# A mixer whose attention rows of two chunks are turned in slot 11, with the output products begun beside the first scores

## What is computed

```python
def parallel_mixer(x, pos, w_in, gate_bias, conv_w, conv_b, sink, att_g, mlstm_g, w_out):
    u = x @ w_in
    aq, ak, av = ...          # 8 query heads, 2 key/value heads of 64, rotated in part
    y_att = rms_norm(windowed_gqa(aq, ak, av, sink), att_g)
    y_ml = mlstm_group(u_qk, u_v, u_o, u_gates, ...)   # 4 heads of 128, both directions
    return concatenate([y_att, y_ml], axis=-1) @ w_out
```

## Time and profile before

| what | value |
|---|---|
| time, median of 3 runs | 2205.72 us (2204.82 to 2207.74) |
| time of the profiled execution | 2197.67 us |
| its span | 2196.1 us |
| mean granted clock of TensorE | 0.984 |
| PE busy | 2095.0 us, 10880 matmuls |
| DVE busy | 1318.4 us (60%) |
| ACT busy | 979.1 us (45%) |
| POOL busy | 226.7 us (10%) |

### The profile page before, as it was taken

One profiled execution on the slowest core, in us unless ns is written; L12 is line 12 of the kernel. 1 busy time (PEld: TensorE's weight loads), 2 busy tenths in 40 slices (PEclk: granted clock), 3 DMA queues, 4 the chain that ended last, 5 costly groups with the idle time before them and its releaser, 6 DMA issues.

```text
span 2196.1 us, 30246 instructions
## 1 busy us (share of the span) xinstructions
PE 2095.0 (95%) x10880; PEld 1671.8 (76%) x10880; DVE 1318.4 (60%) x2005; ACT 979.1 (45%) x1570; POOL 226.7 (10%) x268
## 2 busy tenths in 40 slices
PE   7999999999999899999799998999999989999998
PEld 6888767878877677777588886788888767777774
DVE  3785577721455765556868647782335476665567
ACT  3554565232422355455246547523333134555553
POOL 0000032000001321000100002300000042100004
PEclk9999999999999999999899999999999999999999
DMA  4163202321103699999511112123210169999996
GB/s 156 58 226 128 103 30 79 114 86 49 58 29 125 247 367 373 387 383 346 198 59 39 39 39 96 44 112 115 77 58 20 41 228 384 373 375 373 380 382 230
DMA packets 78526, 384.78 MB, mean 175 GB/s; under 512 B 10472, under 2 KB 11864, under 8 KB 43608
## 3 DMA queue, kind: packets, MB, share of 16 engines
q1 hardware_dynamic: 55264, 327.31, 39.5%
q0 software_dynamic: 10096, 30.38, 3.8%
q10 hardware_dynamic: 13064, 25.75, 3.2%
HBM read 352.27 MB, written 46.07 MB: 181 GB/s over the span
## 4 chain that ended last, share of the span: by engine, by line
PE 79%; DVE 12%; ACT 6%; issue 2%; DMA 1%; DVEq 0%; ACTq 0%; POOL 0%; SPq 0%; POOLq 0%
PE bank L2247 32%; PE bank L2781 10%; PE bank L2755 9%; PE bank L2745 7%; PE bank L2482 5%; PE bank L2454 2%; PE bank L2592 2%; PE bank L2513 2%; PE bank L2268 2%; DVE weight_slots_parts L1472 1%; PE bank L2721 1%; PE bank L2636 1%; DVE weight_slots_parts L1953 1%; PE bank L2652 1%; PE bank L2422 1%
## 5 line engine op out<-in xcount | busy, mean ns | idle before, releaser
L1953 DVE TENSOR_TENSOR weight_slots_parts<-weight_slots,mixer_region_parts 128x2048 fp32r<-128x2048 f32 x140 | 323.4, 2330 | 85.1 <-ACT mixer_region_parts L1296 85.0
L2247 PE MATMUL bank<-weight_slots_parts,x_transposed_parts 128*128 128x512 f32 x864 | 278.6, 404 | 1.4 <-DVE weight_slots_parts L1472 1.4
L1296 ACT ACTIVATE mixer_region_parts<-weight_slots 128x2048 fp32r<-128x2048 f32 x140 | 260.9, 1908 | 23.4 <-ACT x_transposed L1371 18.1
L2247 PE MATMUL bank<-x_transposed_parts,weight_slots_parts 128*128 128x512 f32 (+1 forms) x1024 | 260.7, 341 | 3.8 <-DVE mixer_region_parts L1441 2.7
L1472 DVE TENSOR_TENSOR weight_slots_parts<-weight_slots,weight_slots_parts 128x2048 fp32r<-128x2048 f32 x58 | 132.9, 2292 | 197.5 <-ACT weight_slots_parts L981 196.6
L2781 PE MATMUL bank<-weight_slots,x_transposed 128*128 128x512 f32 x560 | 247.6, 595 | 0.0
L2755 PE MATMUL bank<-mixer_region_parts,x_transposed_parts 128*128 128x256 f32 x1120 | 207.5, 284 | 1.1 <-DVE weight_slots_parts L1953 1.1
L2247 PEld LDWEIGHTS bank<-x_transposed_parts,weight_slots_parts 128*128 128x128 f32 x1024 | 178.5, 191 | 25.9 <-issue 3.6
L2745 PE MATMUL bank<-mixer_region_parts,x_transposed_parts 128*128 128x512 f32 x560 | 192.2, 414 | 5.4 <-ACTq L1336 2.4
L2781 PEld LDWEIGHTS bank<-weight_slots,x_transposed 128*128 128x128 f32 x560 | 104.1, 191 | 118.5 <-issue 102.9
L2247 PEld LDWEIGHTS bank<-weight_slots_parts,x_transposed_parts 128*128 128x128 f32 x864 | 162.3, 194 | 33.8 <-DVE weight_slots_parts L1472 2.3
(11 more groups left out here) (322 smaller groups left out, 3525.4 us busy)
## 6 DMA issues: line engine op xcount, KB each, us to landing
weight_slots<-in_w_gate SPq DMA_DIRECT2D x70, 1024.0 KB, 7.4
weight_slots<-in_w_up SPq DMA_DIRECT2D x70, 1024.0 KB, 7.2
weight_slots<-in_w_down SPq DMA_DIRECT2D x70, 1024.0 KB, 8.0
weight_slots<-in_w_in SPq DMA_DIRECT2D x20, 1024.0 KB, 5.2
slots_y<-x_transposed ACTq DMA_DIRECT2D x66, 256.0 KB, 7.2
weight_slots<-in_wkv_mem SPq DMA_DIRECT2D x16, 1024.0 KB, 4.8
slots_y<-in_consts SPq DMA_DIRECT2D x6, 2304.0 KB, 16.9
weight_slots<-in_w_out SPq DMA_DIRECT2D x8, 1024.0 KB, 4.9
```

What stands on the lines that cost most here:

```text
L1296: nc.scalar.activation(hi, raw, ACT.Copy).then_inc(moe.high_ready, 1)
L1953: v.tensor_tensor(lo, raw, hi.bitcast(F32), ALU.subtract).then_inc(moe.low_ready, 1)
L2247: ins = pe.matmul(ps, lhs[i](k), rhs[j](k), start=k == 0 and a == 0, stop=k == KD - 1 and a == 2)
```

## The change

- The scores of three key blocks take four banks, one head of 384 columns in each; there is no second group behind the turned probabilities. The stream tiles have banks 6 and 7 while such slots are ahead.
- Slot 11 has three stream tiles and slot 12 one, ("o", 5, 1), between the spread maxima and the weighing. ScalarE's sigmoid of ("o", 4, 1) moves behind group 0, beside that of ("o", 5, 1).
- The roots are taken in slot 9 for chunks 0 to 2, whose rows are scaled at the end of VectorE's slot 9, and in slot 11 for chunks 3 and 4.
- wo0 is split one tile earlier. Attention rows of chunks 0 and 1 are turned in slot 11 into banks 0 and 1, behind the weighing, and split there.
- Group 0 does two steps of the early sums behind each of its four scores, none behind the first score of group 1, and one at each point from then on. Rows of chunks 2 to 5 are turned in group 0 into banks 5 and 6. VectorE adds nothing to the residual in group 0.

```diff
-PER_SLOT = [3, 3, 2, 3, 3, 2, 4, 4, 4, 4, 4, 4]
+PER_SLOT = [3, 3, 2, 3, 3, 2, 4, 4, 4, 4, 4, 3, 1]
-YT_BEHIND = ((), (0, 1, 2, 3), (4,), (5,))
+YT_AHEAD = (0, 1)
+YT_BEHIND = ((), (2, 3), (4,), (5,))
...
 def score_tiles(i):
-    pairs = ((0, 2), (0, 1)), ((1, 3), (0, 1))
-    return pairs if keys_of(GROUP_ORDER[i][0])[1] == 2 else pairs + (((0, 1, 2, 3), (2,)),)
+    return ((0, 2), (1, 3)) if keys_of(GROUP_ORDER[i][0])[1] == 2 else ((0,), (1,), (2,), (3,))
 def stream_banks(i):
-    return (3, 6, 7) if any(len(score_tiles(n)) == 3 for n in range(i, 12)) else (2, 3, 6, 7)
+    return (6, 7) if any(len(score_tiles(n)) == 4 for n in range(i, 12)) else (2, 3, 6, 7)
...
 def early_steps(point):
-    return max(0, ML_POINTS.index(point) + 1 - CHUNKS[0])
+    at = ML_POINTS.index(point)
+    ahead = 4 * len(YT_AHEAD)
+    return min(2 * at + 2, ahead) if at <= CHUNKS[0] else min(ahead + at - CHUNKS[0], EARLY_STEPS)
...
-                add(("sc", i, b), (b,))
+                add(("sc", i, b), (0, 1, 2, 3) if len(score_tiles(i)) == 4 else ((0, 1)[b],))
...
+        for c in YT_AHEAD if i == 11 else ():
+            add(("yt", c, 0), (0, 1))
...
-                    add(("yt", c, 0), (4, 5, 6, 7))
+                    add(("yt", c, 0), (5, 6))
...
+SPLIT_BEHIND[("o", 5, 0)] = SPLIT_BEHIND.pop(("o", 3, 1))
...
# ScalarE
-                        if i == 11:
-                            rstd(st[:, 20:25], st[:, 20:25], 5, 1.0 / ATT, eps_rms).then_inc(att_rs, 1)
+                        if i in (9, 11):
+                            lo, hi = (20, 23) if i == 9 else (23, 25)
+                            rstd(st[:, lo:hi], st[:, lo:hi], hi - lo, 1.0 / ATT, eps_rms).then_inc(att_rs, 1)
...
                             stream_tile(t)
+                            if t == STREAM[STARTS[11]]:
+                                for c in YT_AHEAD:
+                                    high_x(("yt", c, 0), c, 0)
...
-                                    for c in ((), (0, 1), (2, 3, 4), (5,))[sc]:
+                                    for c in ((), (2,), (3, 4), (5,))[sc]:
                                         high_x(("yt", c, 0), c, 0)
                         if g == 0:
+                            stream_tile(STREAM[-2])
                             stream_tile(STREAM[-1])
...
# VectorE
                         if i == 12:
-                            dve.wait_ge(att_rs, 2 * l + 1)
-                            for c in range(NC - 1):
+                            dve.wait_ge(att_rs, 3 * l + 2)
+                            for c in (3, 4):
                                 attention_scaled(c)
...
                         for t in w[1:]:
                             stream_tile(t)
+                            if t == STREAM[STARTS[11] + 1]:
+                                for c in YT_AHEAD:
+                                    low_y(c, 0)
+                        if i == 9:
+                            dve.wait_ge(att_rs, 3 * l + 1)
+                            for c in range(3):
+                                attention_scaled(c)
...
-                        done_ = early_steps(ML_POINTS[at - 1]) // 4 if at else 0
+                        done_ = early_steps(ML_POINTS[at - 1]) // 4 if point[0] else 0
...
                         if g == 0:
+                            tile_finish(len(STREAM) - 2)
                             tile_finish(len(STREAM) - 1)
...
# TensorE
-                        if i < 12 and nb == 3:
-                            tile_filled(pe, ("pt", i - 1, 0))
-                            scores(2, 1)
-                            scores(2, 3)
+                        if i == 12:
+                            unit_ready("running_max")
+                            spread_maxima(0)
                         if w and i:
                             stream_tile(w[0])
...
+                        for c in YT_AHEAD if i == 11 else ():
+                            pe.wait_ge(y_att, 6 * l + c + 1)
+                            turn4(("yt", c, 0), lambda k: y[:, c, k * P:(k + 1) * P])
                         for t in w[1 if i else 2:]:
                             stream_tile(t)
```

More of the change, by code:

```diff
@@ L135 @@
           + [(name, c, h) for name in ("v", "o") for c0 in (0, 3) for h in range(2) for c in range(c0, c0 + 3)])
-PER_SLOT = [3, 3, 2, 3, 3, 2, 4, 4, 4, 4, 4, 4]
-STARTS = [sum(PER_SLOT[:i]) for i in range(13)]
+PER_SLOT = [3, 3, 2, 3, 3, 2, 4, 4, 4, 4, 4, 3, 1]
+STARTS = [sum(PER_SLOT[:i]) for i in range(14)]
 GATES_TURNED = 8
@@ L1600, in stream_tile @@
                             dve.sem_inc(o_ready, 1)
-                        if i:
+                        if i and key != STREAM[-1]:
                             tile_finish(i - 1)
@@ L1721, in _ @@
                                 if g == 0 and sc == 1:
-                                    dve.wait_ge(att_rs, 2 * l + 2)
+                                    dve.wait_ge(att_rs, 3 * l + 3)
                                     attention_scaled(NC - 1)
                                 if g == 0:
-                                    for c in ((), (0, 1), (2, 3), (4, 5))[sc]:
+                                    for c in ((), (2,), (3, 4), (5,))[sc]:
                                         low_y(c, 0)
@@ L2413, in _ @@
                             tiles = score_tiles(i)
-                            def scores(b, t):
+                            for t in range(GRP):
                                 n, j = head_at(jp, t)
                                 hp = slice(n * HD, (n + 1) * HD)
-                                heads, blocks = tiles[b]
-                                key, at, m = ("sc", i, b), heads.index(t), len(blocks) * P
-                                lo = (k0 + blocks[0]) * P
+                                b = t % len(tiles)
+                                key, at = ("sc", i, b), tiles[b].index(t)
                                 ps = bank_of(key) if at else take(key)
-                                ins = pe.matmul(ps[:, at * m:(at + 1) * m], qT[hp, j, c * P:(c + 1) * P],
-                                                kT[hp, lo:lo + m], start=True, stop=True)
-                                if t == heads[-1]:
+                                ins = pe.matmul(ps[:, at * nb * P:(at + 1) * nb * P], qT[hp, j, c * P:(c + 1) * P],
+                                                kT[hp, k0 * P:(k0 + nb) * P], start=True, stop=True)
+                                if t == tiles[b][-1]:
                                     done(ins, key)
-                            for t in range(GRP):
-                                scores(t % 2, t)
-                            if nb == 3:
-                                scores(2, 0)
-                                scores(2, 2)
                         if i:
```

16 lines of the change are left out of this document (6 added, 10 removed).

## The result

The changed kernel takes 2217.30 us (median, 2212.61 to 2218.35) against 2203.06 of the kernel before: ratio 1.006, 95% interval 1.0044 to 1.0076, or +9.7 to +16.7 us. It is slower, as forecast, but by some 13 us where the prediction had 6.6: twice as much. The forecast of 2212.3 looks nearer than that because it was added to 2205.72, a median of three runs, and the kernel before takes 2203.06 over six. The profiled execution took 2218.35 us.

The account below looks back on a forecast made before the run. TensorE, busy 95%, was taken as the bound, with ScalarE and VectorE setting the pace behind slot 11. -4.8 + 5.35 + 3.65 - 2.8 + 3.4 + 1.8 = +6.6 us, added to 2205.72: 2212.3; range 2204 to 2219.

Parts of the forecast that it names:

- The new wait: Ninth early-sum step, group 0: TensorE stands 6.9 us for VectorE's residual of tile (0, 0), behind decays and two sigmoids.
- The clock behind it: After the idle time at the ninth step the granted clock falls: 1.7 us a layer, +3.4; ends 0 and double.
- Third numerator: Group 0's third numerator tile comes later through TensorE's idle time: +5.35 us in layer 1, +3.65 in layer 0.
- Scores: Slots 2 to 5: four products of 384 columns save 0.6 us a slot, -4.8 over both layers.
- one more pair: Slots 9 to 11: extra tiny ScalarE operations, with three VectorE scalings, are hidden in busy stretches; without that cover 2.3 us.
- Row maxima: Slots 11 and 12: maxima wait about 0.9 us for VectorE's split turned rows, where a wait of 1.4 was.
- the later loads of x: SP's loads of x, wo2 and wo3 start 3 us later, at about 1330: costs nothing, without margin up to 3.
- The tail: Behind group 6's last numerators: TensorE idles about 5 us; -1.4 a layer for earlier output, +0.9 a layer for the clock.
- VectorE starts 1.4 earlier, and so does the first output product: After the last numerators, VectorE's half of wo2 and the first output product come earlier: -1.4 us a layer, -2.8.
- The wait decides, the clock does not: Rival, 25%: everything as forecast but granted clock at 1.00: +1.4 us, 2207.1, within 0.2%.
- The steps fill the gap: Rival, 10%: short wait at the ninth step, -10.6 us or 2195.1; decides once ScalarE's chain is 7 us shorter.
- Low clock for longer: Rival, 10%: twice the forecast's clock terms, 2217.5 us.

Follow-up runs that it names:

- The late sigmoids: Changed kernel with ScalarE's sigmoids of the last two o tiles, and VectorE's products using them, put behind the decays of group 1: ratio 1.0005.
- the filled wait: Changed kernel with 28 needless products of 512 columns ahead of the ninth step, keeping TensorE busy while it would wait: ratio 1.0019.
- the scores alone: Kernel before with only the scores changed (four products of three key blocks, a bank each, stream on two banks): ratio 0.9976, again 0.9974.

## Why the prediction was right, and where its sizes were off

Forecast 2212.3, slower; measured 2217.3, slower, inside the range. The mechanism was the forecast's, the new wait and the low clock behind it; the sum was half of what came. That the time lies within the range is luck in part: the base to which the +6.6 was added was 2.7 us too high, and on a base of 2203.06 the same range would have ended at 2216.3.

| part, both layers | forecast, us | measured, us |
|---|---|---|
| up to slot 11 (scores, slot 9) | -4.8 | -3.3 |
| slot 11 to third numerator (wait, clock) | +12.4 | +16.2 |
| behind it (tail, clock) | -1.0 | +0.3 |
| sum | +6.6 | +13.25 |


- **The new wait.** Forecast 6.9 us, at the ninth step, for the residual of tile (0, 0), in both layers: measured 6.98 and 6.98. Each link of the chain was there in the forecast's order. From slot 11's start TensorE reached the step 0.8 later than forecast (32.84 against 32.01 in layer 1) and ScalarE ended its last high part 0.7 later (32.05 against 31.31), so both ends moved together and the wait kept its size: that it was right to 0.1 is luck, that it was near 7 is not. Of TensorE's 0.8 the prediction's own addition explains 0.3 (1327.5 + 0.7 + 2.8 + 1.7 is 1332.7, not 1332.4). The late sigmoids show the link that matters.
- **The clock behind it** was the term most undersized: 1.7 forecast, from the 2.72 us wait of the earlier trace rows, and 2.9 and 2.6 measured by filling the wait. The idle time here is two and a half times as long, and I took the price of the shorter one. The term lay within its stated ends (0 to double).
- **Third numerator.** With both, +7.05 in layer 1 and +5.35 in layer 0 were forecast from slot 11's start, and +9.14 and +7.06 came: 1.2 and 0.9 of the difference from the clock, 0.9 and 0.8 from the chain being later.
- **Scores.** Forecast -2.4 a layer, measured -2.2 by the end of slot 5: slots 2, 4 and 5 give 0.8 each, and slot 3 gives 0.25 back. There the third turned tile waits for ScalarE's copy of the first, 1.05 us longer than before: TensorE's part of slot 2 has become 0.8 shorter, the chain of VectorE and ScalarE through it has not, and ScalarE comes to the copies 2.1 us behind the first turn instead of 1.1. First the row of the kernel before, then that of the changed one:

```profile
119.20 0.66 PE L2407 MATMUL bank<-constants,scratch 128*128 128x128 f32 x4 [0.64 <-ACT scratch L941]
```

```profile
121.36 0.66 PE L2424 MATMUL bank<-constants,scratch 128*128 128x128 f32 x4 [1.68 <-ACT scratch L946]
```

- **Slot 9.** The sum had nothing here. The "one more pair" of tiny operations on ScalarE, which it called "hidden", was the step that failed: the pair takes 0.57 and stood ahead of ScalarE's half of a weight split on which VectorE and TensorE wait (TensorE waits 0.57 longer in layer 1, 0.69 in layer 0), and slot 11 began 1.6 to 1.7 earlier instead of 2.4. ScalarE's share of 8.87 in 14.80 us said that it had time, not what was queued behind the pair.
- **Row maxima.** Forecast a wait of 0.9 for the split rows where one of 1.4 was for copies: measured 0.82. Nothing waited for the later loads of x.
- **The tail.** Forecast -1.4 a layer and +0.9 for the clock, so -0.5; measured -0.20 and +0.52. Of "VectorE starts 1.4 earlier, and so does the first output product" the first half came nearly true and the second did not. Counted from the last group-6 numerator, VectorE's half of wo2 began at 8.31 before the change (1423.74) and at 7.22 after, 1.1 earlier in layer 1 (1.2 in layer 0); the first output product began only 0.4 earlier (11.38 and 11.02; 0.9 in layer 0). VectorE's half took 2.57 instead of 2.29, and the 16 turns ahead of the product took 3.68 instead of 1.97 at the low clock, so that now the product stands behind the turns. Up to the group-6 numerator 0.2 and 0.6 were lost, and 0.5 and 0.3 in the output products, of which the first run at the low clock. The rows of the kernel before (those of the changed one stand under "The tail" above):

```profile
1415.43 1.28 PE L2513 MATMUL bank<-mixer_region 128*128 128x129 f32 x10
...
1423.37 1.97 PE L2268 MATMUL bank<-constants,mixed 128*128 128x128 f32 x16 [0.47 <-POOL mixed L841]
1426.81 0.72 PE L2482 MATMUL bank<-weight_slots_parts,x_transposed_parts 128*128 128x512 f32 x2 [1.48 <-DVE mixed_parts L1441]
```

  The wait for GpSimd, forecast at 4 to 5, was 3.99 and 3.89.
- **Rivals.** "The wait decides, the clock does not" is excluded by the filled wait. "The steps fill the gap" needed ScalarE's chain 7 us shorter; taking two sigmoids (4.15) out of it brought the wait to 2.82, the remainder that this condition leaves. "Low clock for longer" (10%, 2217.5) came nearest in time, and its clock terms (3.4 a layer behind the wait) were nearer to the 2.9 and 2.6 than my 1.7. Its hit on the time is luck in part, as it rests on the same high base (+11.8 where +13.25 came). I had given the larger chance to the price of a shorter wait.

## What to carry to other kernels

Before work is moved forward, ask which resource it takes back, and from whom. Here the ninth step needed a bank, the bank a residual on VectorE, the residual two products ahead of it, the products the decays, and the decays stood in a queue behind two sigmoids that nobody needed yet. The repair that shortened the wait was not at the bank but at the head of that queue. Where an in-order engine's share of busy time is low, a tiny instruction is still not free if something late is queued right behind it.
And price an idle stretch of TensorE with the clock behind it, from a row of a wait as long as itself, and with ends: equal waits had different prices here.

## What the runs showed of the hardware that I had not expected

- Filling 6.4 us of waiting with 28 products that nobody reads made the stretch 6 us shorter, though the ninth step started where it had (218.58 and 218.75): the granted clock behind it was 1.00 instead of 0.57.
- The same wait has different prices. Behind 1.42 us for ScalarE's copies in layer 1 the granted clock stayed at 1.00 before the change and was 0.50 over 5 us with the scores alone; in layer 0 it was 0.55 over 5 us already before the change. Behind 0.83 us it was 1.00; behind 1.63 us it was 0.66 in one version and 1.00 at the same place in the next. After 6.97 and 6.98 us the third numerator came 1.35 us apart in two runs of one program. What decides between these is open.
- The stretches that the change leaves alone vary by 8 to 9 us between profiles (730.0 to 738.1, 732.2 to 741.7), some ten times what the changed stretch, as a sum over both layers, does between two runs of one program (673.38 twice, 657.41 and 658.22). A layer alone moves by more: 1.5 us between the two runs of the scores alone. A single span would have told 20.6 us here for a change of 13.
